# Mix projection of a streaming encoder layer: three pairs of output tiles in a row by block products, in place of two pairs with plain tiles between

## What is computed

```python
y_a = o_sb.reshape(B, T, SB_W) @ w_proj_sb
y_b = o_mla.reshape(B, T, MLA_OW) @ w_proj_mla
mix = (jax.nn.sigmoid(gate_a) * y_a + jax.nn.sigmoid(gate_b) * y_b) @ w_out   # 1024 x 1024
x = x + rmsnorm(mix, g_post_mix)
u = rmsnorm(x, g_pre_ffn) @ w_up
...
f = (jax.nn.gelu(gate, approximate=True) * val) @ w_down                       # 2816 x 1024
x = x + rmsnorm(f, g_post_ffn)
```

## Time and profile before

| | us |
|---|---|
| median of 3 runs | 1813.55 |
| lowest, highest | 1813.34, 1813.96 |
| the profiled execution | 1813.86 |
| span of its trace | 1812.0 |

### The profile page before, as it was taken

One profiled execution on the slowest core, in us unless ns is written; L12 is line 12 of the kernel. 1 busy time (PEld: TensorE's weight loads), 2 busy tenths in 40 slices (PEclk: granted clock), 3 DMA queues, 4 the chain that ended last, 5 costly groups with the idle time before them and its releaser, 6 DMA issues.

```text
span 1812.0 us, 34936 instructions
## 1 busy us (share of the span) xinstructions
PE 1796.0 (99%) x13958; PEld 1736.5 (96%) x13958; DVE 1169.2 (65%) x2036; ACT 778.1 (43%) x1585; POOL 1105.0 (61%) x1364
## 2 busy tenths in 40 slices
PE   9999999999999999999999999999999999999999
PEld 8998989999999999999999988899999999999999
DVE  6677675445778568554657767753657795785554
ACT  4444453235556245332344444532365552552321
POOL 8676634548555845957666865345475558459384
PEclk9999999999999999999999999999999999999999
DMA  5342211324222222323342421122242223223232
GB/s 186 96 120 80 77 42 59 105 94 146 77 87 93 94 84 92 96 75 101 106 144 91 139 77 59 56 74 82 89 148 82 82 94 94 94 85 103 73 94 97
DMA packets 76465, 170.55 MB, mean 94 GB/s; under 512 B 6608, under 2 KB 34384, under 8 KB 76304
## 3 DMA queue, kind: packets, MB, share of 16 engines
q1 hardware_dynamic: 68976, 160.79, 28.0%
q10 hardware_dynamic: 7328, 7.54, 1.3%
HBM read 156.41 MB, written 9.79 MB: 92 GB/s over the span
## 4 chain that ended last, share of the span: by engine, by line
PE 88%; DVE 8%; ACT 1%; issue 1%; POOL 1%; DMA 0%; SPq 0%; DVEq 0%; POOLq 0%; ACTq 0%
PE ps L2153 56%; PE ps L2557 9%; PE ps L2193 4%; PE ps L2643 3%; PE ps L2321 3%; PE ps L2279 2%; PE ps L2576 1%; DVE R L1483 1%; PE ps L2232 1%; PE ps L2375 1%; PE ps L2381 1%; DVE xn L1483 1%; DVE RF L1785 1%; PE ps L2593 1%; PE ps L2298 1%
## 5 line engine op out<-in xcount | busy, mean ns | idle before, releaser
L2153 PE MATMUL ps<-xn,wsp 128*128 128x272 f32 x7728 | 989.8, 289 | 2.6 <-ACT R L1127 0.8
L2153 PEld LDWEIGHTS ps<-xn,wsp 128*128 128x128 f32 x7728 | 973.9, 189 | 8.0 <-issue 3.0
L836 POOL TENSOR_TENSOR wsp<-raw,wsp 128x256 fp32r<-128x256 f32 x440 | 346.4, 809 | 17.6
L822 POOL TENSOR_TENSOR wsp<-raw,wsp 128x256 fp32r<-128x256 f32 x216 | 158.8, 769 | 178.3 <-ACT wsp L1012 178.3
L831 POOL CAST wsp<-raw 128x512 fp32r<-128x512 f32 x220 | 151.6, 689 | 179.8 <-DMA raw<-in_wstream 124.1
L1483 DVE SCALAR_TENSOR_TENSOR R<-ps,R 128x512 fp32r<-128x512 f32 (+13 forms) x272 | 129.5, 499 | 64.6 <-ACT R L931 19.0
L810 POOL TENSOR_TENSOR wsp<-raw,wsp 128x512 fp32r<-128x512 f32 x80 | 121.9, 1545 | 67.4 <-DVE raw L1785 43.1
L817 POOL TENSOR_TENSOR wsp<-raw,wsp 128x256 fp32r<-128x256 f32 x136 | 100.9, 775 | 83.0 <-ACT wsp L1012 83.0
L2153 PE MATMUL ps<-R,wsp 128*128 128x272 f32 x960 | 124.8, 290 | 0.1
L2153 PEld LDWEIGHTS ps<-R,wsp 128*128 128x128 f32 x960 | 121.7, 189 | 1.4 <-DVE xT L1512 0.5
L2557 PE MATMUL ps<-R,wsp 128*128 128x272 f32 x816 | 110.3, 290 | 2.7 <-POOL wsp L810 2.5
(11 more groups left out here) (304 smaller groups left out, 2728.1 us busy)
## 6 DMA issues: line engine op xcount, KB each, us to landing
raw<-in_wstream SPq DMA_DIRECT2D x233, 512.0 KB, 3.6
raw<-in_wstream SPq DMA_DIRECT2D x48, 128.0 KB, 2.6
raw<-in_wstream SPq DMA_DIRECT2D x16, 384.0 KB, 3.2
xT<-in_x_in SPq DMA_DIRECT2D x16, 272.0 KB, 4.3
raw<-in_kc SPq DMA_DIRECT2D x8, 512.0 KB, 3.5
raw<-in_vc SPq DMA_DIRECT2D x8, 512.0 KB, 4.5
out_k_out<-mix ACTq DMA_DIRECT2D x8, 272.0 KB, 3.0
out_y_out<-xT ACTq DMA_DIRECT2D x1, 2176.0 KB, 9.6
```

The source lines that it names most:

```text
L822: ins = nc.gpsimd.tensor_tensor(dst[:, 1, f], part[:, f], dst[:, 0, f].bitcast(F32), ALU.subtract)
L836: ins = nc.gpsimd.tensor_tensor(dst[:, 1, f], part[:, f], dst[:, 0, f].bitcast(F32), ALU.subtract)
L2153: mm = pe.matmul(z[:, h], w[:, x, (k0 + k) * P:(k0 + k + 1) * P], rhs[:, y, k, h * HT:(h + 1) * HT], start=(k == 0 and (x, y) == (0, 0)), ...
```

## The change

In the mix projection, tiles 3 and 6 become a third pair. The order is now tile 0, pairs (1, 4), (2, 5), (3, 6) directly behind one another, tile 7. `plain_out` goes, and the stream of weights and the places of their loads among SyncE's other transfers follow the new order. For pairs 2 and 3, VectorE makes the low parts of S1 and S3 (`sum_low`, with a semaphore `sum_lo` of its own), so that GpSimd has four left: A11, A22, S2, A12. On VectorE the sums S1, S2 and S3 and both low parts of the next pair stand ahead of the joins of the pair at work, and S4 behind them; on ScalarE the high parts of the next pair are spread among the copies of the pair at work. GpSimd's wait for `mi_lo` moves from ahead of A11 of the first pair to ahead of its S1.

In part 0 of the down projection ScalarE now copies P5, P2 and P4 to SBUF and VectorE only joins P7 and P3, as in the mix projection.

```diff
-BLOCK_PAIRS = {OUT: [(1, 4), (2, 5)], ...}
+BLOCK_PAIRS = {OUT: [(1, 4), (2, 5), (3, 6)], ...}
+ON_VECTOR = [(OUT, j, n) for j in range(1, len(BLOCK_PAIRS[OUT])) for n in ("S1", "S3")]
+def pool_lows(i, j):
+    if (i, j, "S1") in ON_VECTOR:
+        return ["A11", "A22", "S2", "A12"]
+    return list(DOWN_LOWS)
...  SyncE
-                    load_to(ST_AT[("out", 2)])
+                    load_to(ST_AT[("out", 5)])
-                    behind = {1: ("out", 5), 2: ("out", 6), 3: ("out", 7), 5: ("pp", 0)}
+                    behind = {1: ("out", 3), 2: ("out", 6), 3: ("out", 7), 5: ("pp", 0)}
...  GpSimd
-                            if (i, j) == (OUT, 0):
-                                pool.wait_ge(S["mi_lo"], M_LO[KT - 1, "B"])
-                            for n in DOWN_LOWS:
+                            for n in pool_lows(i, j):
+                                if (i, j) == (OUT, 0) and n == "S1":
+                                    pool.wait_ge(S["mi_lo"], M_LO[KT - 1, "B"])
...  ScalarE, mix projection
                         if j > 0:
                             hand_on(OUT, j, "P1", "P2")
-                        keep_product("P5", j, a, 1)
+                        if more:
+                            plain_high(OUT, j + 1, ("A11",))
+                        keep_product(OUT, "P5", j, a, 1)
                         hand_on(OUT, j, "P6", "P3")
-                        cast(("out", OUT_PLAIN[j]))
-                        keep_product("P2", j, a)
+                        if more:
+                            plain_high(OUT, j + 1, ("A22",))
+                            sum_high(OUT, j + 1, "S1")
+                        else:
+                            cast(("pp", 0))
+                        keep_product(OUT, "P2", j, a)
                         hand_on(OUT, j, "P7", "P4")
+                        if more:
+                            sum_high(OUT, j + 1, "S2")
+                            sum_high(OUT, j + 1, "S3")
                         act.wait_ge(S["dve_read"], dread(("P3", OUT, j)))
-                        square(0, 3 * j + 1, fT[:, a])
+                        square(0, 2 * j + 1, fT[:, a])
                         if more:
-                            plain_high(OUT, j + 1, ("A11",))
+                            sum_high(OUT, j + 1, "S4")
...  ScalarE, part 0 of the down projection (and the same with P2 and P4)
+                            if i == 0:
+                                keep_product(0, "P5", j, j, 1)
                             hand_on(i, j, "P6", "P3")
...  VectorE
                     for j, (a, b) in enumerate(BLOCK_PAIRS[OUT]):
-                        add_squares(0, 3 * j)
-                        join_products("P7", j, b, a)
-                        join_products("P3", j, a, a)
-                        if j < len(BLOCK_PAIRS[OUT]) - 1:
-                            for n in SUMS:
+                        more = j < len(BLOCK_PAIRS[OUT]) - 1
+                        if more:
+                            for n in ("S1", "S2", "S3"):
                                 weight_sum(OUT, j + 1, n)
+                            sum_low(OUT, j + 1, "S1")
+                        for m in (2 * j - 1, 2 * j) if j > 0 else (0,):
+                            add_squares(0, m)
+                        if more:
+                            sum_low(OUT, j + 1, "S3")
+                        join_products(OUT, "P7", j, b, a)
+                        join_products(OUT, "P3", j, a, a)
+                        if more:
+                            weight_sum(OUT, j + 1, "S4")
                             last_low(OUT, j + 1)
+                            if i == 0:
+                                join_products(0, "P7", j, j + NP, j)
+                                join_products(0, "P3", j, j, j)
...  TensorE
                     for j in range(len(BLOCK_PAIRS[OUT])):
                         for n in ("P1", "P5", "P6", "P2", "P7", "P3", "P4")[j == 0:]:
                             down_product(n, OUT, j)
-                        plain_out(OUT_PLAIN[j])
```

More of the change, by code:

```diff
@@ L38 @@
 OUT = -1
-OUT_PLAIN = [3, 6]
-BLOCK_PAIRS = {OUT: [(1, 4), (2, 5)], **{i: [(j, j + NP) for j in range(NP)] for i in range(LAST)}}
+BLOCK_PAIRS = {OUT: [(1, 4), (2, 5), (3, 6)], **{i: [(j, j + NP) for j in range(NP)] for i in range(LAST)}}
 PAIR_ORDER = [(i, j) for i in BLOCK_PAIRS for j in range(len(BLOCK_PAIRS[i]))]
@@ L85 @@
 STREAM += [("proj", j) if n == "ya" else (n, j) for n, j in MIXES if n != "yb"]
-OUT_ORDER = [0] + [m for pair, plain in zip(BLOCK_PAIRS[OUT], OUT_PLAIN) for m in (*pair, plain)] + [KT - 1]
+OUT_ORDER = [0] + [m for pair in BLOCK_PAIRS[OUT] for m in pair] + [KT - 1]
 STREAM += [("out", j) for j in OUT_ORDER] + [("pp", 0)] + FFN
@@ L100 @@
 UP = ("upg", "upv")
-CAST = STREAM[ST_AT[("proj", 2)]:ST_AT[("out", 0)] + 1] + [("out", j) for j in OUT_PLAIN + [KT - 1]] + [("pp", 0), ("upg", 0)]
+CAST = STREAM[ST_AT[("proj", 2)]:ST_AT[("out", 0)] + 1] + [("out", KT - 1), ("pp", 0), ("upg", 0)]
 CAST += [c for n, c in enumerate(STREAM) if c[0] in UP and STREAM[n - 6][0] in UP]
@@ L413, in build @@
         EVENTS += [("open", ("out", 0)), ("turn", OUT), *block_products(OUT, 0)[:2], ("done", ("out", 0)), *block_products(OUT, 0)[2:]]
-        for j, plain in enumerate(OUT_PLAIN):
-            if j > 0:
-                EVENTS += block_products(OUT, j)
-            whole(("out", plain))
+        for j in range(1, len(BLOCK_PAIRS[OUT])):
+            EVENTS += block_products(OUT, j)
         by_halves(("out", KT - 1), ("half", 0))
@@ L500, in readers @@
                 return 0, t[1]
-            if t[0] in ("P2", "P4", "P5") and t[1] == OUT:
+            if t[0] in ("P2", "P4", "P5") and t[1] in (OUT, 0):
                 return 1, 0
@@ L656, in build @@
             pre = {n: st.enter_context(nc.semaphore(n)) for n in
-                   ("con_in", "late_in", *(f"x_in{k}" for k in range(KT)), "c_in", "y_done0", "y_gate0", "y_raw0", "qr_in", "made", "cast", "x_st", "x_back", "p_in", "conv_st", "squares", "added", "summed", "logs", "roots", "sum_raw", "sum_hi",
+                   ("con_in", "late_in", *(f"x_in{k}" for k in range(KT)), "c_in", "y_done0", "y_gate0", "y_raw0", "qr_in", "made", "cast", "x_st", "x_back", "p_in", "conv_st", "squares", "added", "summed", "logs", "roots", "sum_raw", "sum_hi", "sum_lo",
                     "y_st")}
@@ L2561, in down_product @@
                             mm.then_inc(S["p_done"], 1)
-                    def plain_out(m):
-                        t = ("out", m)
-                        banks_free(t)
-                        w, z = wsp[:, ring_slot(layer, t)], ptile(t)
-                        for k in range(KT):
-                            if k == KT - 1 and m == 0:
-                                down_product("P1", OUT, 0)
-                            split(t, k, k == 0)
-                            if m == 0:
-                                pe.wait_ge(S["mi_lo"], M_LO[k, "B"])
-                            for x, y in PARTS:
-                                for h in range(2):
-                                    mm = pe.matmul(z[:, h], w[:, x, k * P:(k + 1) * P], mix_plain(k, y)[:, h * HT:(h + 1) * HT],
-                                                   start=(k == 0 and (x, y) == (0, 0)), stop=(k == KT - 1 and x == 1), skip_group_check=True)
-                        mm.then_inc(S["p_done"], 1)
-                    plain_out(0)
+                    t = ("out", 0)
+                    banks_free(t)
+                    w, z = wsp[:, ring_slot(layer, t)], ptile(t)
+                    for k in range(KT):
+                        if k == KT - 1:
+                            down_product("P1", OUT, 0)
+                        split(t, k, k == 0)
+                        pe.wait_ge(S["mi_lo"], M_LO[k, "B"])
+                        for x, y in PARTS:
+                            for h in range(2):
+                                mm = pe.matmul(z[:, h], w[:, x, k * P:(k + 1) * P], mix_plain(k, y)[:, h * HT:(h + 1) * HT],
+                                               start=(k == 0 and (x, y) == (0, 0)), stop=(k == KT - 1 and x == 1), skip_group_check=True)
+                    mm.then_inc(S["p_done"], 1)
                     for j in range(len(BLOCK_PAIRS[OUT])):
```

94 lines of the change are left out of this document (53 added, 41 removed).

## The result

| | before | after |
|---|---|---|
| median (12 runs each) | 1813.64 | 1817.96 |
| lowest, highest | 1813.1, 1814.8 | 1816.57, 1820.09 |
| profiled execution, its span | 1813.86, 1812.0 | 1817.02, 1815.2 |

The ratio is 1.0022, with an interval of 1.0015 to 1.0029: the changed kernel is slower by 4.3 us. The forecast was 1810.6 us, with a range up to 1814.0 us.

What follows compares the result with a forecast made beforehand. TensorE, busy 99% of the span, was taken as the bound. Per layer -1.60 + 0.55 + 0.55 - 1.0 = -1.5 us, -3.0 for both, giving 1810.6 us; own range 1809.2 to 1812.2, wider range 1808.0 to 1814.0.

Steps and rivals of the forecast that it cites:

- The matmuls: Mix projection: two plain tiles (12.12 us) give way to one pair of 10.52 us, -1.60 us a layer.
- The break moves from P1 to P6 of pair 1: Mix projection: GpSimd's earlier A11 ends P1's wait but holds VectorE's sum of both branches, delaying P6; +0.55 us a layer.
- The turn to pair 2: Mix projection, pair 1 to 2: P6 waits for S2's low part, behind S4 on VectorE; +0.55 us a layer, bounds 0 and 2.1.
- The turn to pair 3: Mix projection, pair 2 to 3: same chain needs 5.2 us of 6.0 available; no cost, 0.8 us to spare.
- Other moved steps, at nothing: GpSimd's low parts, SyncE's queue, buffer releases, tile 7's cast and the last squares all in time; no cost.
- Part 0: Down projection: taking copies off VectorE lets S4 and S2's low part come earlier; -1.0 us a layer, bounds 0 and 1.18.
- The clock: TensorE's clock was read as granted in full throughout the profile before; no term for it in the sum.
- Rival C: Mix projection: S4 chain on VectorE late at both turns by two held periods, 2.1 us each; +2.15 a layer, 1817.85 us; chance 0.07.

Runs made afterwards that it cites:

- part 0 alone: Kernel before with only ScalarE's copies and VectorE's joins in part 0 of the down projection; 1811.01 us, ratio 0.9984.
- hand-on ahead: Changed kernel with ScalarE's copy of the next pair's P1 moved right behind its copy of P4; 1812.81 us, ratio 0.9994 to the kernel before.
- the made gap: Kernel before plus two activation table loads on ScalarE ahead of the first hand-on of P1; 1820.05 us, ratio 1.0034.

## Why the prediction was wrong, point by point

- **The matmuls** (-1.60 us a layer): right.
- **The break moves from P1 to P6 of pair 1** (+0.55): right in kind and cause, a little small. I had P6 near 415.8 us and it began at 415.70, behind the hand-on at 415.22. VectorE's sum of both branches took 1.37 us in place of 0.72, as forecast. Against 415.27 us, with the start of the stage 0.24 us earlier, the loss is 0.67. The prediction set the Trainium skill's rule (SBUF — State Buffer, "Who interferes with whom"), by which the later of the two instructions blocks until the first has finished, against rows in which an operation lasted 1.05 us longer and GpSimd's took 1.30. That was a misreading. This trace agrees with the rule: GpSimd's A11 ran from 406.65 to 407.94 us, and VectorE's sum, begun at 407.15, ended at 408.52, 0.58 us behind it. It lasts less than 1.3 us longer because it begins after GpSimd's instruction has. The loss of 0.67 us lies between my 0.55 and the 0.75 that I had worked out for holding until A11 is over.
- **The turn to pair 2** (+0.55): this is the step that failed, here and at the turn to pair 3: P6 was taken to wait for S2's low part alone. The chain that I followed was right to a tenth: I had S2's low part ready at 427.0, or 426.8 with the earlier start, and it was ready at 426.77. But P6 also waits for the copy of P1, and I followed only one of its two producers. I named the joins and the squares on VectorE and never read ScalarE's new queue past the high parts of S2 and S3. It could have been read blind: from my own 424.9 for the end of both joins, two squares, S4's high part, the copy of P4 and the hand-on are some 2.6 us (2.55 in the trace after), which gives 427.5 and makes P6 1.1 us late. Measured was 1.20; the run with the copy ahead left 0.57, so 0.63 us was the copy's place.
- **The turn to pair 3** (0, "0.8 us to spare"): failed for the same reason and one more. Measured was 2.02 us late. S2's low part came 6.4 us behind the end of P7 in place of my 5.2, which alone would have made P6 0.4 late; the other 1.6 us is ScalarE's queue, with the cast of tile 7 in it as well. And the queue began late, since the joins came 2.1 us after P3 was done: VectorE's S1 low part was held (1.76 us), then two squares took 2.64, then S3's low part. I had allowed one held period.
- **Other moved steps, at nothing**: the tile 7 cast was written down as "one pair ahead of its use". It was, but I asked only whether it was in time, not what stood behind it.
- **Part 0** (-1.0): right in kind, too small. It gave 1.36 and 1.44 us, past my bound of 1.18, since part 0 came out 0.2 us shorter than part 1; by itself it gave 3 us in two layers. No hand-on came late there.
- **The clock** (not in the sum): I had read it as granted in full in the trace of before and took that for given. Behind the new breaks it falls in most executions. It fits what lies between the 3.2 us of the two traces, both at full clock, and the 4.3 us of the medians: the three executions of the kernel after at 1.000 took 1817.02 to 1817.09 us, the nine below it 1818.24 in the median.
- **The stretch between the layers** (not in the sum): +1.36 us, of which 1.1 in the norms and the first projections of layer 2.

By layer: -1.60 (matmuls) + 0.67 + 1.20 + 2.02 = +2.3 in the mix projection, against 2.4 measured and -0.5 forecast. Rival C named the right side, nearly the right time (1817.85) and the right turns, but put the delay into the chain of S4 on VectorE, held by GpSimd. That chain alone would have cost 0.5 and 0.4 us at the turns. That C's time fits is luck: it has 4.2 us at the two turns where 3.2 were measured, and it has neither the stretch between the layers nor the clock. The holding was only part of the cause: VectorE's work made the joins late, and ScalarE's order turned late joins into a late P6. Either repair alone removes most of the delay at the turns, which is why moving one copy (5.1 us) and taking VectorE's low parts away (5.5 us) each bring back nearly the same microseconds.

What stays open is the stretch between the layers, where no code was changed. From part 2's last group to layer 2's group of 684 it took 385.4 to 385.7 us in the kernel before, part 0 alone, hand-on ahead and the made gap, and 386.1 to 387.3 us in all the others. TensorE's timeline of the kernel after has two breaks there that before doesn't have:

```profile
865.13 16.08 PE L2229 MATMUL ps<-xn,wsp 128*128 128x272 f32 x126 [0.53 <-DVE xn L1498]
...
887.46 2.74 PE L2189 MATMUL ps<-xn,wsp 128*128 128x272 f32 x20 [0.24 <-POOL wsp L841]
```

The first comes after a VectorE operation that took 1.26 us in place of 0.71 beside a GpSimd instruction, so it looks like the same holding, met or missed by how the queues happen to stand. No run tested that. Kernels with the same code there differ by up to 2 us, so a forecast that leaves this stretch out can be off by as much.

## What to carry to other kernels

When a change takes away the work that lay between two groups, list for each product all that it waits for (weights' low part, bank, handed-on sum) and walk the whole queue of every engine that makes one of them, up to the instruction itself; the latest sets the start, and a short copy at the end of an in-order queue is as dangerous as a long sum. Put the copies that release TensorE ahead of those steps on the same engine which wait for a third engine. When a break closes, look for the next chain behind it: here, with the break at P6 of pair 1 gone, delays stood at pairs 2 and 3, and only with the chain of S2's low part cleared as well did the stage get shorter.

## What the hardware showed that I had not expected

A single break of some 2 us in a run of matmuls that is otherwise unbroken was often followed by a fall of the granted clock. Behind 7 of the 18 such breaks that the traces hold (2.04 to 2.47 us), the 36 matmuls took 6.05 to 6.11 us, at a mean granted clock of 0.72 or 0.73, in place of 4.56: the break cost 1.5 us more than its own length. Behind the other 11 the clock stayed full, once with the same break in the other layer of the same execution. In traces with no break above 1.25 us in this stage the clock stayed full.
